# Last attention of a two-block model: probabilities normalized ahead of the transposes, values stationary, outputs split straight from PSUM

## What is computed

```python
def gqa_attend(q, k, v, sink=None):          # q (b, t, 8, 128), k and v (b, 768, 2, 128)
    s = einsum('bqhgd,bkhd->bhgqk', q, k) * d ** -0.5
    p = softmax(s, axis=-1)
    o = einsum('bhgqk,bkhd->bqhgd', p, v)
y_lat = o.reshape(b, 512, 1024) @ w_out
x = x + mod_l[:, :, 2] * y_lat
```

## Time and profile before

| | |
|---|---|
| median of 3 runs | 3195.48 us (3192.57 to 3196.05) |
| the profiled execution's own time | 3196.6 us |
| its span, first to last instruction | 3194.8 us |
| PE (matmul) busy | 3025.9 us, 95% |
| DVE busy | 1626.7 us, 51% |
| ACT busy | 1223.6 us, 38% |
| mean granted TensorE clock | 0.974 |

### The profile page before, as it was taken

The page is one execution under the profiler, slowest core; times in us unless marked ns, Lnnn a source line. Parts: engine busy times, 40 slices in busy tenths (PEclk is TensorE's granted clock), DMA queues, the critical chain, the costliest instruction groups (busy, mean ns, idle before and its releaser), DMA issues.

```text
span 3194.8 us, 39955 instructions
## 1 busy us (share of the span) xinstructions
PE 3025.9 (95%) x15336; PEld 2420.6 (76%) x15336; DVE 1626.7 (51%) x2502; ACT 1223.6 (38%) x2040; POOL 154.3 (5%) x142
## 2 busy tenths in 40 slices
PE   7979999999999999999998889999999899899999
PEld 5657778867767778767886657888888776778887
DVE  4874677774454677675227453333333634343344
ACT  3443333335554333335124443332222434443333
POOL 2200000011000000010003001000000100000000
PEclk9979999999999999999998999999999999999999
DMA  5102443433201443421220001121121120022221
GB/s 196 54 14 79 158 164 138 184 108 59 73 28 65 167 174 136 166 86 53 53 79 1 1 1 53 53 79 53 55 77 53 53 78 2 8 91 87 105 87 71
DMA packets 159714, 259.24 MB, mean 81 GB/s; under 512 B 54316, under 2 KB 74154, under 8 KB 159468
## 3 DMA queue, kind: packets, MB, share of 16 engines
q1 hardware_dynamic: 157844, 252.66, 22.7%
q10 hardware_dynamic: 1628, 4.78, 0.4%
q0 software_dynamic: 128, 0.26, 0.0%
HBM read 255.59 MB, written 2.10 MB: 81 GB/s over the span
## 4 chain that ended last, share of the span: by engine, by line
PE 83%; DVE 7%; ACT 4%; issue 2%; DVEq 2%; ACTq 0%; POOLq 0%; DMA 0%; PEldq 0%; PEld 0%
PE psA L790 23%; PE psA L791 22%; PE psA L792 22%; PE psA L747 3%; PE psB L761 2%; ACT work L1324 2%; PE psA L911 2%; PE psO L931 1%; PE psO L878 1%; PE psA L1000 1%; DVE psA L2008 1%; ACT w_hi L1324 1%; PE psA L806 1%; DVE work L2152 1%; PE psA L808 1%
## 5 line engine op out<-in xcount | busy, mean ns | idle before, releaser
L1324 ACT ACTIVATE w_hi<-wbuf 128x1024 fp32r<-128x1024 f32 (+1 forms) x349 | 368.2, 1057 | 1176.1 <-PE psA L792 1150.1
L790 PE MATMUL psA<-act_hi,w_hi 128*128 128x512 f32 (+1 forms) x1872 | 708.9, 379 | 45.3 <-DVE act_lo L2040 31.6
L2034 DVE TENSOR_TENSOR w_lo<-wbuf,w_hi 128x1024 fp32r<-128x1024 f32 (+1 forms) x349 | 430.6, 1236 | 555.6 <-ACT w_hi L1324 551.4
L791 PE MATMUL psA<-act_lo,w_hi 128*128 128x512 f32 (+1 forms) x1872 | 699.9, 374 | 0.0
L792 PE MATMUL psA<-act_hi,w_lo 128*128 128x512 f32 (+1 forms) x1872 | 698.9, 373 | 0.0
L790 PE MATMUL psA<-hid_hi,w_hi 128*128 128x512 f32 (+1 forms) x1280 | 477.4, 373 | 5.5 <-DVE work L2152 4.5
L791 PE MATMUL psA<-hid_lo,w_hi 128*128 128x512 f32 (+1 forms) x1280 | 472.3, 369 | 0.0
L792 PE MATMUL psA<-hid_hi,w_lo 128*128 128x512 f32 (+1 forms) x1280 | 471.5, 368 | 0.0
L790 PEld LDWEIGHTS psA<-act_hi,w_hi 128*128 128x128 f32 x1872 | 357.5, 191 | 116.8 <-issue 40.6
L791 PEld LDWEIGHTS psA<-act_lo,w_hi 128*128 128x128 f32 x1872 | 357.6, 191 | 62.6 <-issue 2.6
L792 PEld LDWEIGHTS psA<-act_hi,w_lo 128*128 128x128 f32 x1872 | 356.9, 191 | 62.4
(11 more groups left out here) (293 smaller groups left out, 3381.6 us busy)
## 6 DMA issues: line engine op xcount, KB each, us to landing
wbuf<-in_mlp_w_dram SPq DMA_DIRECT2D x64, 2048.0 KB, 8.1
work<-in_ada_w_dram SPq DMA_DIRECT2D x32, 1536.0 KB, 11.1
wbuf<-in_ab_w_in_dram SPq DMA_DIRECT2D x10, 1024.0 KB, 5.1
wbuf<-in_ple_w_gate_dram SPq DMA_DIRECT2D x4, 2048.0 KB, 8.0
wbuf<-in_c_w_in_dram SPq DMA_DIRECT2D x3, 2048.0 KB, 7.9
wbuf<-in_hy_w_in_dram SPq DMA_DIRECT2D x2, 2048.0 KB, 11.0
wbuf<-in_hy_w_out_dram SPq DMA_DIRECT2D x2, 2048.0 KB, 7.9
wbuf<-in_mla_w_out_dram SPq DMA_DIRECT2D x2, 2048.0 KB, 8.6
```

What stands on the lines that cost most here:

```text
L790: pe.matmul(psA[:, s, a:b], w_hi, x_hi[:, a:b], start=first, stop=False)
L791: pe.matmul(psA[:, s, a:b], w_hi, x_lo[:, a:b], start=False, stop=False)
L1324: return nc.scalar.activation(out, in_, func, **kw)
L2034: tt(split_target(wL, stage, u), unit(v, stage, u, g), split_target(wH, stage, u), ALU.subtract).then_inc(S["w_split"], 1)
```

## The change

- The units come in another order: heads 0 to 3 for all four query blocks, then heads 4 to 7. Four units make a "row" of 4 heads and one query block; there are eight rows.
- DVE inverts each unit's sum as soon as the exponential is there and multiplies the 128x768 probabilities by it, in place (`normalize`). PE's transposes wait for that (`cat_normed`).
- In the value product the values are stationary and the turned probabilities move, so the result in psO has features on the partitions. Rows use the two halves of psO in turn.
- When a row is complete, ACT rounds its 128x512 from PSUM to `act_hi` (`row_hi`), and DVE writes the rest to `act_lo` (`row_lo`). After rows 3 and 7 `act_split` rises by 4.
- The final transposes, the copies to `mixT3` and `on3`, and `finish` are gone. The first two tiles of the projection's weights are split during units 20, 21 and 24, 25.

The diff, cut (of the old function bodies only the first line stands):

```diff
@@ -89,7 +89,7 @@
 ROW_H = 4
 PLAN_B = [("load", 17), ("vi", 1), ("dsa", 4 * DSA_H), ("mla", 4 * MLA_H), ("cols", 1), ("ka", 6), ("va", 6), ("vb", 2),
           ("sw", 8 * B_H), ("hs", 8),
-          ("cat", 2 * LT * C_H), ("cat_o", 8), ("out", 8)]
+          ("cat", 2 * LT * C_H), ("out", 8)]
 
 
 
...
-        mixT3 = area(KD, LAT, at=0)
         qC, vC, kC = area(KD, LAT, at=3 * KD * TOK), area(6, 256, at=4 * KD * TOK), area(C_KV, TOK, at=0)
         sqc, rsc = area(4, TOK), area(2, TOK)
         assert cursor[0] <= KD * TOK
         rtc = area(2, LAT, at=3 * KD * TOK + KD * LAT)
-        prob3, turn3 = area(2, TOK, at=KD * TOK), area(2, TOK)
-        on3 = area(LT, D, at=3 * KD * LAT)
+        prob3, turn3 = area(2, TOK, at=3 * KD * LAT), area(2, TOK)
 
...
@@ -605,11 +601,20 @@
         def units(name):
 
             s, at, r = ATT[name], 0, []
-            for qt in rows_of_queries(name):
-                for h in range(s["H"]):
-                    r.append((len(r), qt, h, at))
-                    at += len(turned_groups(name, qt))
+            order = [(qt, h) for qt in rows_of_queries(name) for h in range(s["H"])]
+            if name == "cat":
+                order = [(qt, h0 + e) for h0 in range(0, C_H, 4) for qt in range(LT) for e in range(4)]
+            for qt, h in order:
+                r.append((len(r), qt, h, at))
+                at += len(turned_groups(name, qt))
             return r
+
+        def cat_row(row):
+
+            _, qt, h0, _ = units("cat")[4 * row]
+            at = 512 * (row % 2)
+            part = (slice(None), slice(h0, h0 + 4), slice(qt * P, qt * P + P))
+            return psO[:, at:at + 512].rearrange("p (e q) -> p e q", q=P), sH[LAT][part], sL[LAT][part]
...
@@ -858,43 +863,35 @@
                             S["sum_ready"], 1)
                 return add
 
-            def attention(name, beside=None):
-                s = ATT[name]
-                us = units(name)
+            def cat_attention():
+                us = units("cat")
 
                 def turn_probs(u, qt, h, b0):
-                    emptied(pe, name, u)
-                    for g, kbs in enumerate(turned_groups(name, qt)):
-                        turn(name, b0 + g, [((kb - kbs[0]) * P, s["prob"][:, u % 2, kb * P:kb * P + P]) for kb in kbs])
+                    pe.wait_ge(S["cat_normed"], u + 1)
+                    for g, kbs in enumerate(turned_groups("cat", qt)):
+                        turn("cat", b0 + g, [((kb - kbs[0]) * P, prob3[:, u % 2, kb * P:kb * P + P]) for kb in kbs])
 
                 def weigh_values(u, qt, h, b0):
-                    for g in range(len(turned_groups(name, qt))):
...
+                    for g in range(2):
+                        turned(pe, "cat", b0 + g)
+                    row, kv = u // 4, h // (C_H // C_KV)
+                    if u % 4 == 0 and row >= 2:
+                        pe.wait_ge(o_free, n_o["cat"] + row - 1)
+                    at = 512 * (row % 2) + u % 4 * P
+                    for kb in range(6):
+                        ins = pe.matmul(psO[:, at:at + P], vC[:, kb, kv * P:kv * P + P], turn3[:, u % 2, kb * P:kb * P + P],
+                                        start=(kb == 0), stop=(kb == 5))
+                    if u % 4 == 3:
                         ins.then_inc(o_ready, 1)
 
                 for step in range(len(us) + 2):
-                    if beside:
-                        beside[0](step)
                     if step < len(us):
                         u, qt, h, _ = us[step]
-                        product(name, u, s["logits"](qt, h))
+                        product("cat", u, cat_logits(qt, h))
                     if 0 <= step - 1 < len(us):
                         turn_probs(*us[step - 1])
-                    if beside:
-                        beside[1](step - 1)
                     if step >= 2:
                         weigh_values(*us[step - 2])
-                pe.wait_ge(S["onat_set"], n_o[name] + s["QT"])
-                for t in range(s["H"] * s["dv"] // P):
-                    turn(name + "_o", t, [(qt * P, s["onat"](qt)[:, t * P:t * P + P]) for qt in range(LT)])
 
             def attention_ahead(name):
                 s = ATT[name]
@@ -1312,7 +1309,7 @@
             c_rotate(8)
             c_rotate(9)
             meet(pe)
-            attention("cat")
+            cat_attention()
             split_linear("c_out", sH[LAT], sL[LAT], LAT, split_here("c_out"), behind=mean_square_of(3, "c_out"))
             mlp("mlp3", 3, LAT)
             meet(pe)
@@ -1379,6 +1376,34 @@
                     if u >= 1:
                         evacuate(*us[u - 1])
                 evacuate(*us[-1])
+            def cat_attention():
+                us = units("cat")
+
+                def evacuate(u, qt, h, b0):
+                    for g, kbs in enumerate(turned_groups("cat", qt)):
+                        ps, free = get_b(act, "cat", b0 + g)
+                        f(turn3[:, u % 2, kbs[0] * P:(kbs[-1] + 1) * P], ps[:, 0:len(kbs) * P], ACT.Copy).then_inc(free, 1)
+
+                def row_hi(row):
+                    total, hi, _ = cat_row(row)
+                    act.wait_ge(o_ready, n_o["cat"] + row + 1)
+                    f(hi, total, ACT.Copy).then_inc(S["act_hi"], 1)
+
+                for u, qt, h, b0 in us:
+                    c = qt * C_H + h
+                    act.wait_ge(S["cat_max"], u + 1)
+                    slot, _ = A("cat", u)
+                    f(prob3[:, u % 2, :], psA[:, slot, 0:TOK], ACT.Exp, bias=nmax[:, c:c + 1],
+                      accum_out=rsum[:, c:c + 1]).then_inc(a_free[slot], 1)
+                    if u >= 1:
+                        evacuate(*us[u - 1])
+                    if u % 4 == 2 and u >= 6:
+                        row_hi(u // 4 - 1)
+                    if u in (20, 24):
+                        w_hi("c_out", (u - 20) // 4)
+                evacuate(*us[-1])
+                row_hi(len(us) // 4 - 1)
+
             def split_hi(x, x_hi, n):
 
                 for k in range(KD):
@@ -1815,14 +1840,7 @@
                     c_root(n - 3)
             c_root(9)
             meet(act)
-            attention("cat")
-            for n in range(C_H):
-                ps, free = get_b(act, "cat_o", n)
-                f(mixT3[:, n, :], ps, ACT.Copy).then_inc(free, 1)
-                act.drain()
-                f(sH[LAT][:, n, :], mixT3[:, n, :], ACT.Copy).then_inc(S["act_hi"], 1)
-                if n < 2:
-                    w_hi("c_out", n)
+            cat_attention()
             split_linear("c_out", square_of("c_out", LAT), start=2)
             rms(3, 1, 3, LAT, hraw, sH[LAT], ahead=[("mlp3", 0), ("mlp3", 1)])
             mlp("mlp3", 3, LAT)
@@ -1928,49 +1946,35 @@
                 stt(r, r, 1.0, s, ALU.add, ALU.mult)
                 v.drain()
 
-            def attention(name, beside=None):
...
+            def cat_attention():
+                us = units("cat")
+
+                def normalize(u, qt, h, b0):
+                    c = qt * C_H + h
+                    emptied(v, "cat", u)
+                    nc.vector.reciprocal(rinv[:, c:c + 1], rsum[:, c:c + 1])
                     v.drain()
-                    for h in range(H):
...
+                    ts(prob3[:, u % 2, :], prob3[:, u % 2, :], rinv[:, c:c + 1], None, ALU.mult).then_inc(S["cat_normed"], 1)
+
+                def row_lo(row):
+                    total, hi, lo = cat_row(row)
+                    v.wait_ge(S["act_hi"], BASE_X["c_out"] + row + 1)
+                    tt(lo, total, hi, ALU.subtract).then_inc(o_free, 1)
+                    if row % LT == LT - 1:
+                        v.drain().then_inc(S["act_split"], 4)
+
+                for u, qt, h, b0 in us:
+                    c = qt * C_H + h
+                    if u >= 1:
+                        normalize(*us[u - 1])
+                    ps, _ = get_a(v, "cat", u)
+                    nc.vector.tensor_reduce(nmax[:, c:c + 1], ps[:, 0:TOK], AX.X, ALU.max, negate=True).then_inc(S["cat_max"], 1)
+                    if u % 4 == 3 and u >= 7:
+                        row_lo(u // 4 - 1)
+                    if u in (21, 25):
+                        w_lo("c_out", (u - 21) // 4)
+                normalize(*us[-1])
+                row_lo(len(us) // 4 - 1)
 
             def attention_ahead(name, beside=None):
                 s = ATT[name]
@@ -2656,8 +2660,8 @@
                 c_turn(i - 1)
             c_turn(9)
             meet(v)
-            attention("cat")
-            gated("c_out", 1, LAT, mixT3)
+            cat_attention()
+            gated("c_out", 1, LAT)
             rms(3, 1, "norm2", 3, LAT, hraw, "mlp3", ahead=[("mlp3", 0), ("mlp3", 1)])
             mlp("mlp3", 3, LAT)
             meet(v)
```

(58 more changed lines are left out.)

## The result

The changed kernel takes 3179.86 us (median of five runs, 3175.16 to 3180.58) beside 3193.94 us of the kernel before (five, 3192.57 to 3196.05): a ratio of 0.9949 with the interval 0.9938 to 0.996, or -16.3 us (-19.8 to -12.8); the two medians by themselves are 14.1 us apart. A second set of runs (experiment e8) gave 0.9945 (0.9929 to 0.9962). The forecast, 3182.1 us against 3195.48, is a ratio of 0.9958 and lies inside both intervals, but 3 to 4 us short of their middles. Against this comparison's time of before, 0.9949 is 3177.7 us, 0.8 us under the low end of the range (3178.5); the median of the five runs, 3179.86, lies above it.

The account below looks back on a forecast made before the run. PE's gapless chain was taken to bound the kernel, 3.29 us a unit. Terms (a) to (h) sum to -13.4 us, so 3195.5 becomes 3182.1 us (chance 0.68); range 3178.5 to 3188.5.

Parts of the forecast that it names:

- (d): Steady loop: reciprocal and multiplication ahead of PE's transposes, 1.05 us, just fit by 0.03 us; +0.5 us, bounds 0 and 1.5.
- (f): Units 21 and 25: the weights' rest on DVE behind the maxima makes normalization late, twice; +0.35 us.
- (a): Inside the stage: finish goes, three times 0.9 us; row_hi and row_lo in its place cost nothing; -2.7 us.
- (b): Stage end: no finish, transposes or copies; projection starts right behind the last value product, hiding row 7's split; -12.7 us.
- (g): Stage end: nothing hides the last unit's normalization, so its transposes come later; +0.45 us.
- (c): Projection's start: PE doesn't idle before it, so the first five matmuls aren't slow; -1.1 us.
- (e): First units: no room for normalization, and unit 0's division stands ahead of unit 1's maximum; +1.8 us.
- (h): Value product: stationary values need the same six products and as many weight loads; price 0.
- B: Loop rival: the in-place multiplication takes 1.03 us instead of 0.62, late every second unit; 3188 us, chance 0.13.
- C: First units, rival: new idle time makes PE's clock fall to 1.2 GHz, 2.5 to 3 us; 3185, chance 0.10.
- D: Projection rival: early start fails because something in its first tiles waits; 3184 to 3186 us, chance 0.05.
- E: Loop rival: normalization isn't hidden, each of 32 units pays 1.05 us; slower than before, 3213 us, chance 0.03.

Follow-up runs that it names:

- e8: The changed kernel itself, unmodified, timed again in six runs beside the kernel before: 3179.07 us, ratio 0.9945.
- e1: Changed kernel without the division (outputs not normalized; transposes wait for the exponential only): 3177.36 us.
- e2: Changed kernel with the projection's tiles 0 to 3 announced after row 7 instead of after row 3, so no early start: 3182.43 us.
- e3: Changed kernel with the division's multiplication as a slower operation with a second tensor operand, same values: 3180.98 us.
- e6: Changed kernel with DVE taking unit 1's maximum ahead of unit 0's division, nothing else: 3180.58 us.
- e7: e6 plus 2 + 2 unread matmuls around the last rotation ahead of the stage to keep PE's clock up: 3176.32 us, ratio 0.9944.
- e4: Changed kernel with a second in-place multiplication, by 1.0, behind the division's first: 3191.29 us.
- e5: Kernel before with only the division ahead of the transposes added; finish (multiplying by 1), unit order, final transposes and copies stay: 3198.56 us, ratio 1.0013.

## Why the prediction was right or wrong

The direction, the mechanism and each large term held. The sum was some 1 us too small on the stage and what follows (-13.4 for -14.5), and two terms that should have been nothing, (d) and (f), are 0.85 us of that. The profiled spans differ by another 2.2 us ahead of the stage, for which the sum had nothing. The range left too little for both together.

- **(a) finish inside the stage**, -2.7: the 28 distances fell from 94.79 to 92.05 us, **-2.74**, and are even (3.28 or 3.29).
- **(b) and (g), the end**, -12.7 + 0.45: 18.70 to 6.24, **-12.46** in all; e1 gives (g) as 0.34. e2 shows the early start as 1.80 us of it.
- **(c) the projection's slow first matmuls**, -1.1: 2.24 to 1.23, **-1.0**. In the window of the earlier trace rows, 2764.00 to 2776.20, PE is now in the projection, busy 11.02 of 12.2 us at a mean clock of 1.00.
- **(d) the division in the loop**, +0.5, and **(f) the weights' rest**, +0.35: **zero** both. This is the step that failed. "It just fits, by 0.03 us" was worked out from hand-overs added up one by one, with 0.28 us for reciprocal and drain and 0.12 from DVE to PE; they take 0.24 and 0.06 us here, and e3 puts the room at some 0.11. Then a loss was priced for a miss that doesn't happen. For (f) the distances behind units 21 and 25 are 3.29 like the others. The sum added up shown durations, 0.96 and 1.24 us, but DVE's next instruction starts before the shown end of the one ahead: behind unit 21 the maximum starts at 2721.68, the weights' rest at 2722.56 and the reciprocal at 2723.70, 2.02 us behind the maximum and not 2.20, which is when the exponential is ready anyway.
- **(e) the start**, +1.8: **+1.98** (e1: 1.96). The chain given for it, division ahead of the second maximum, is what the trace shows. The other order brought nothing in e6, whose second logits ran at half clock, and some 1.2 us at full clock (e7).
- **(h) values stationary**, 0: the twelve records took 1.35 us before and take 1.34 now (2702.41 to the next logits at 2703.75).
- **The rest**, 0 in the sum: -2.2 us of the profiled difference lie ahead of max 0, -0.3 behind the projection's start. This is the larger part of the distance between the forecast and the profiles, and its cause stays open. The range had 2.5 us for this together with the spread of runs. But runs of one program spread more: before, 3185.24 to 3201.37 in seventeen runs, and the faster ones had the higher mean clock (0.977 at 3185.24, 0.972 at 3201.37).

The rivals. **B** is refuted as a fact: 620 ns in place. The rule of the Trainium skill ("VectorE: DVE Perf Modes", section "Mode 2×_2P — use both read ports for one tensor") speaks of an output that partially overlaps its input, as invalid for the fast mode in the compiler's check; the trace shows that a multiplication exactly in place runs at the pace of L2172's 618 ns, not at the 1.02 us of e3. B's price was about right: +5.4 us of stage in e3 for a forecast of +6. **C**: the clock was low in the first units, as it was before, but didn't fall again (0.51, 0.63, then 1.00 from 2656). With longer chains (e3, e4) it does fall again, but its price of 3 us isn't seen, as all but some 0.1 us of e3's longer start is explained by its longer multiplications. The Trainium skill's rule that transposes don't count ("TensorE: Matmul & The Clock Gate", section "Part 4: PE-mode transpose") changed nothing in the loop: the mean clock from 2660 to 2760 us is 1.00, with transposes a fifth of PE's time. The prediction also read rows 4 as agreeing with this rule; they don't bear on it, for what PE ran ahead of that fall were the rotations (L1302, `psO<-work,const` 128x512), ordinary matmuls and no transposes. **D** is refuted, and e2 is what it would have been. **E** is refuted in the loop; its mechanism, units one behind the other, is true of the first two alone. e4 shows that even 0.69 us more costs only 0.27 a unit.

Still open: what sets the moment at which the clock falls ahead of the stage, where the 2.2 us come from, and which of the two mechanisms limits e4.

## What to carry to other kernels

Scaling early can pay although it is more work: not by itself (e5 loses 4 us), but where it frees a result from an operation at the end, so that the result leaves in the layout the next stage reads. Before pricing a new link in a chain, find when its consumer really needs it; if it comes in time, even by a tenth of a microsecond, it costs nothing in the loop and shows only where the pipeline fills and drains (here 2.3 us). And cut both traces at marks of the stage that changed: here the stage repeats to 0.01 us, while whole runs of one program spread by 16. An order that brings nothing while something else is slow (e6) can pay once that is gone (e7), so write down the clock of both traces before calling a theory refuted.

## What was unexpected of the hardware

- The time of PE's clock falling isn't fixed by the program: in the changed kernel's two profiles the windows 2648 to 2652 us show 1.00 in one and 0.50 in the other.
- 1.55 us without a matmul in front of the projection (e2) left the clock at 2.4 GHz, while in the kernel before the projection's first matmuls ran at half the pace behind 12 us of thin work (PE busy 6.50 of 12.20).
- The same multiplication of 768 columns is 0.62 us with a scalar from memory, 0.56 with the constant 1.0 (e4's second, L1959), and 1.02 with a second tensor operand:

```profile
2700.68 0.62 DVE L1957 TENSOR_SCALAR work<-work,small 128x768 f32<-128x768 f32 x1
2701.38 0.56 DVE L1959 TENSOR_SCALAR work<-work 128x768 f32<-128x768 f32 x1
```
